# Softmax normalisation moved from the attention stage into the head of the merge, three logits tiles, keys loaded in quarters

## What is computed

```python
logits = jnp.einsum('bqgrd,bqkgd->bqgrk', q_b, k_sel).astype(jnp.float32) * att_scale
logits = jnp.where(valid[:, :, None, None, :], logits, NEG_INF)
p = jax.nn.softmax(logits, axis=-1)
return jnp.einsum('bqgrk,bqkgd->bqgrd', p.astype(v.dtype), v_sel)
...
gated = sigmoid(ga) * (y_att @ w_proj_att) + sigmoid(gm) * (y_mlstm @ w_proj_mlstm)
```

## Time and profile before

| | us |
|---|---|
| median of 3 runs | 3803.0 (3801.41 to 3805.9) |
| the profiled execution | 3799.4, span of the instructions 3797.8 |
| attention stage, first instruction to last result stored | about 1246 to 2107 |
| head of the merge | about 2107 to 2153 |

### The profile page before, as it was taken

How to read it: one execution, slowest core, us unless ns; L and a number is a source line. 1 busy time by engine, 2 the same in 40 slices (tenths; PEclk the granted TensorE clock), 3 DMA queues, 4 the chain that set the end, 5 groups by cost and what they waited for, 6 DMA issues and landing times. The chain is left out here.

```text
span 3797.8 us, 45544 instructions
## 1 busy us (share of the span) xinstructions
PE 3048.0 (80%) x12949; PEld 2294.5 (60%) x12950; DVE 2570.2 (68%) x3878; ACT 1789.7 (47%) x2406; POOL 478.1 (13%) x638
## 2 busy tenths in 40 slices
PE   3898699799999467878799495888179999999970
PEld 2766578587687234544455384767157777777760
DVE  4467689789899477767664333121379998989974
ACT  6222466585785223333333322121067777777750
POOL 0111110100000312111111000000311111111103
PEclk7999899999999689989899797888589999999995
DMA  2222322122122544333222454332067979667868
GB/s 99 71 63 72 101 78 83 53 77 83 53 74 68 120 102 92 94 98 78 75 66 46 154 173 151 105 120 90 24 223 255 352 281 352 225 245 262 304 241 354
DMA packets 347250, 537.33 MB, mean 141 GB/s; under 512 B 31508, under 2 KB 188404, under 8 KB 345588
## 3 DMA queue, kind: packets, MB, share of 16 engines
q1 hardware_dynamic: 314372, 422.80, 35.4%
q0 software_dynamic: 30448, 104.61, 7.4%
q10 hardware_dynamic: 2304, 8.39, 0.5%
HBM read 502.12 MB, written 138.47 MB: 169 GB/s over the span
## 5 line engine op out<-in xcount | busy, mean ns | idle before, releaser
L839 DVE TENSOR_TENSOR e_w_lo<-e_raw,e_w_hi 128x1024 fp32r<-128x1024 f32 x392 | 453.2, 1218 | 0.0
L1518 PE MATMUL x_ps<-h_hi,x_w_hi 128*128 128x512 f32 (+1 forms) x1024 | 402.4, 393 | 0.0
L1518 PE MATMUL x_ps<-h_lo,x_w_hi 128*128 128x512 f32 (+1 forms) x1024 | 401.1, 392 | 0.0
L1518 PE MATMUL x_ps<-h_hi,x_w_lo 128*128 128x512 f32 (+1 forms) x1024 | 400.8, 391 | 0.0
L791 ACT CAST e_w_hi<-e_raw 128x1024 fp32r<-128x1024 f32 x392 | 382.3, 1054 | 0.8 <-PE e_pG L742 0.7
L2218 ACT ACTIVATE t_probT<-t_ST 128x512 f32<-128x512 f32 x272 | 161.7, 595 | 357.7 <-PE t_ST L2064 357.2
L2037 PE MATMUL t_L<-t_k,t_q 128*128 128x512 f32 (+3 forms) x320 | 200.0, 665 | 147.2 <-DVE t_max_part L2243 112.1
L1708 DVE TENSOR_SCALAR_CACHE_REDUCE x_relu<-x_score,x_cand 128x1024 uint8<-128x1024 f32 (+3 forms) x217 | 315.6, 1486 | 3.6
L1621 ACT ACTIVATE x_relu<-x_score,x_cand 128x896 int8<-128x896 f32 (+3 forms) x217 | 281.0, 1296 | 55.5 <-DVE x_cand L1715 55.2
L2072 PE MATMUL t_O<-t_probT,t_v 128*128 128x512 f32 x544 | 298.2, 632 | 3.7 <-DVE t_y L2260 2.1
L2243 DVE CUSTOM_DVE_ANT_0 t_junk<-t_L,t_mask 128x512 bf16<-128x512 f32 (+3 forms) x320 | 186.7, 607 | 140.2 <-PE t_L L2037 138.3
(11 more groups left out here) (392 smaller groups left out, 6374.1 us busy)
## 6 DMA issues: line engine op xcount, KB each, us to landing
e_raw<-in_w_exp_gate SPq DMA_DIRECT2D x392, 256.0 KB
e_raw<-in_w_exp_up SPq DMA_DIRECT2D x392, 256.0 KB
e_raw<-in_w_exp_down SPq DMA_DIRECT2D x192, 512.0 KB
projT<-x_out SPq DMA_DIRECT2D x124, 256.0 KB, 2.7
slot_out<-e_y POOLq DMA_DIRECT2D x48, 512.0 KB, 5.9
b_gate<-projT SPq DMA_DIRECT2D x32, 512.0 KB, 5.2
x_w_raw<-in_w_in SPq DMA_DIRECT2D x31, 512.0 KB
x_t<-in_x SPq DMA_DIRECT2D x16, 512.0 KB
```

Of the source, the lines that this page charges most:

```text
L839: nc.vector.tensor_tensor(w_lo[:, u, :], raw[:, u, :], w_hi[:, u, :].bitcast(F32), ALU.subtract).then_inc(gl, 1)
L1518: last = nc.tensor.matmul(ps[0:w, u % 4, :], wt[:, m % 2, kk, 0:w], ht[:, kk, q * 512:(q + 1) * 512], start=(kk == 0 and s == 0), stop=(kk ...
```

## The change

- The value tile keeps 64 columns and one of ones, so `t_O` has 65 rows. It is one tile instead of two. At the end of a step ACT copies it (`out(s)`, behind the exponential of the next step's first unit) to one of three tiles `t_out`, and SP stores the 64 rows unnormalised (two DMAs) and the row of sums (one DMA) to DRAM, for each step, one unit later. `outputs` is gone from DVE.
- In the merge, the sums of all heads are loaded as one tile of 128x128, inverted at once, stored, and loaded again as `b_inverse`, each head's row repeated over 64 partitions (2 DMAs, 64x4x2048 each). The recurrence's four slices are taken first, then the attention's, which DVE multiplies with `b_inverse` before ACT's cast.
- `t_L` has three tiles, and PE may be three parts ahead of DVE.
- Keys and values are loaded in four quarters of 512 keys: the first before the second queries, the second at the end of the initial loads, the others at units 3 and 7. The stage's first loads are queries and keys, not gates. POOL fills one row of `t_k_shift` instead of 64, in two pieces.
- The gates' arithmetic moves from ahead of the units into units 0 to 14, and so do the waits for the convolution's weights. Chunks start at unit 32 instead of 30. Of a chunk, part of DVE's normalisation moves from offset 9 to 8, the transposes from 12 to 13, the result from 13 to 14, its store from 14 to 15. The first eight convolution units stand 2 to 3 units apart instead of 2.

```diff
@@ merge_branches @@
+    ORDER = [4, 5, 6, 7, 0, 1, 2, 3]
@@ sync @@
+            sp.dma_start(SUM[:, :], pg.d["exp_sums"]...).then_inc(sum_in, 16)
+            for at, k in enumerate(ORDER):
+                if at >= 2:
+                    sp.wait_ge(y_l, at - 1)
                 src = pg.d["y_attT" if k < 4 else "y_mlT"]
                 sp.dma_start(yr[:, k % 2, :], src[:, k % 4, :]).then_inc(y_in[k % 4], 16)
+                if at == 1:
+                    sp.wait_ge(rec_ok, 1)
+                    sp.dma_start(rec_d..., SUM[:, :]).then_inc(rec_st, 16)
+                    sp.wait_ge(rec_st, 16)
+                    for z in range(2):
+                        sp.dma_start(REC[z * AD:(z + 1) * AD, :, :], rec_d[z::2, :].partition_broadcast(AD)).then_inc(rec_in, 16)
@@ vector @@
+            dve.wait_ge(sum_in, 16)
+            nc.vector.reciprocal(SUM[:, :], SUM[:, :]).then_inc(rec_ok, 1)
+            for at, k in enumerate(ORDER):
+                if k < 4:
+                    dve.wait_ge(y_in[k], 32)
+                    dve.wait_ge(rec_in, 32)
+                    nc.vector.tensor_tensor(yr[:, k % 2, :], yr[:, k % 2, :], REC[:, k, :], ALU.mult).then_inc(n_ok, 1)
+                dve.wait_ge(y_h, at + 1)
                 nc.vector.tensor_tensor(y_lo[:, k, :], ...).then_inc(y_l, 1)
@@ attend_and_recur @@
-    CHUNK0, PERIOD = 30, 15
-    UNITS_AT = [1 + 2 * m if q == 0 else ...]
+    CHUNK0, PERIOD, NKC = 32, 15, 4
+    UNITS_AT = [1 + 5 * m // 2 if q == 0 else ...]
-        V = sb("v", [P, NT, AKV, P])
+        V = sb("v", [P, NT, AKV, AD + 1])
-        L = c.enter_context(nc.psum_tensor("t_L", [P, 2, 512], F32))
+        L = c.enter_context(nc.psum_tensor("t_L", [P, 3, 512], F32))
-        O = c.enter_context(nc.psum_tensor("t_O", [P, AKV, 512], F32))
+        O = c.enter_context(nc.psum_tensor("t_O", [P, R4, P], F32))
@@ sync @@
-            def store(n):
-                sp.wait_ge(y_ok, 2 * n + 2)
-                sp.dma_start(y_d[:, :, n * P:(n + 1) * P], Y[:, n % 2, :, :]).then_inc(y_st[n % 2], 16)
+            def store(s):
+                n, v = STEPS[s]
+                sp.wait_ge(ou_ok, s + 1)
+                for k in range(2):
+                    sp.dma_start(y_d[k * AD:(k + 1) * AD, 2 * v:2 * v + 2, n * P:(n + 1) * P],
+                                 OU[0:AD, s % 3, k::2, :]).then_inc(y_st[s % 3], 16)
+                sp.dma_start(sum_d[...], OU[AD:AD + 1, s % 3, :, :]).then_inc(y_st[s % 3], 16)
@@ tensor @@
-                if made >= 2:
-                    pe.wait_ge(mx_ok, made - 1)
+                if made >= 3:
+                    pe.wait_ge(mx_ok, made - 2)
@@ values @@
-                if j == 0 and s >= 2:
-                    pe.wait_ge(y_ok, s - 1)
-                nc.tensor.matmul(O[:, v, :], V[:, j, v, :], PT[:, (FIRST[s] + j) % 3, :], ...)
+                if j == 0 and s:
+                    pe.wait_ge(ou_ok, s)
+                nc.tensor.matmul(O[0:AD + 1, :, :], V[:, j, v, :], PT[:, (FIRST[s] + j) % 3, :], ...)
@@ scalar @@
+            def out(s):
+                act.wait_ge(pv_ok, FIRST[s + 1])
+                if s >= 3:
+                    act.wait_ge(y_st[s % 3], 48 * (s // 3))
+                a.copy(OU[:, s % 3, :, :], O[0:AD + 1, :, :]).then_inc(ou_ok, 1)
@@ vector @@
-            def outputs(s):
-                ...
-                v_.reciprocal(RS[:, v, :], O[AD:P, v, :]).then_inc(rs_ok, 1)
```

More of the change, by code:

```diff
@@ L181, in _ @@
         def _(act):
-            for k in range(8):
-                act.wait_ge(y_in[k % 4], 16 * (k // 4 + 1))
+            for k in ORDER:
+                if k < 4:
+                    act.wait_ge(n_ok, k + 1)
+                else:
+                    act.wait_ge(y_in[k % 4], 16)
                 nc.scalar.copy(y_hi[:, k, :], yr[:, k % 2, :]).then_inc(y_h, 1)
@@ L1791, in unit_at, with ended @@
         return UNITS_AT.index(f - off) if f - off in UNITS_AT else None
+    def ended(f, off):
+        return FIRST.index(f - off) - 1 if f - off in FIRST[1:] else None
     with ExitStack() as c:
@@ L1886, in load_chunk, with load_keys @@
                     sp.dma_start(to[:, b, :, :], rows.rearrange("(h c) n -> c h n", c=NT)[k].partition_broadcast(P)).then_inc(x_in[b], 16)
+            def load_keys(q):
+                part = slice(q * 512, (q + 1) * 512)
+                keys = pg.d["k_parts"].rearrange("s (v d) n -> s d v n", d=AD)[:, :, :, part]
+                for k in range(2):
+                    sp.dma_start(KS[k * AD:(k + 1) * AD, :, part].bitcast(F32), keys[k]).then_inc(k_in[q], 16)
+                sp.dma_start(K2[0:AD, :, part].bitcast(F32), keys[0]).then_inc(k_in[q], 16)
+                sp.dma_start(V[:, 4 * q:4 * q + 4, :, 0:AD], pg.d["v"][:, 4 * q:4 * q + 4]).then_inc(v_in[q], 16)
             rows = lambda at: pg.d["projT"][at:at + MH, :].rearrange("h (c n) -> (h c) n", n=P)
+            load(0)
+            load_keys(0)
+            load(1)
             sp.dma_start(gI[:, :], rows(C_IF)).then_inc(g_in, 16)
@@ L2163, in side @@
             def side(f):
-                if f == 7:
+                if f == 1:
+                    act.wait_ge(setup, 1)
+                    act.wait_ge(own_s, 2)
+                    a.activation(ge[:, :], gl[:, :], ACT.Exp, scale=-1.0).then_inc(g_ex, 1)
+                    act.wait_ge(g_ex, 1)
+                    a.activation(gl[:, :], ge[:, :], ACT.Ln, bias=one[:, :]).then_inc(g_ex, 1)
+                if f == 11:
                     act.wait_ge(g_w, 3)
@@ L2220, in _ @@
                         shift_row(s + 1)
+                    if j == 0 and s:
+                        out(s - 1)
                     side(f)
+            out(len(STEPS) - 1)
             for f in range(FLAT, FLAT + 20):
@@ L2378, in _ @@
                         seen, x = seen + 1, x + 1
-                    if j == 0 and s:
-                        outputs(s - 1)
                     if j == n and s + AHEAD < len(STEPS):
```

172 lines of the change are left out of this document (85 added, 87 removed).

## The result

The changed kernel took **3663.64 us** (median of 4 executions, 3660.08 to 3670.41), the kernel before, on the same chip, 3802.2. The ratio is 0.9638, 95% interval [0.9619, 0.9658]: 139 us less, faster, where 99 were forecast (3704 us). The time lies inside the range of 3650 to 3762. The profiled execution took 3666.89 us, its span is 3665.3 us.

What follows compares the result with a forecast made beforehand. PE was the engine to be fed, and DVE mostly failed to feed it. Terms -20 - 34 - 64 - 3 + 22 = -99 from 3799.4 us profiled gave 3700, plus 3.6 for the median: 3704 us, range 3650 to 3762.

Steps and rivals of the forecast that it cites:

- DVE's block at each step's end: Attention steps: a reciprocal of 64x512 and two products, 4.19 us per step, 134 us in all, taken off DVE.
- B: First 32 of 272 attention units (128 keys of one step each): less DVE work and PE idling, -34 us (-20 to -50).
- D: Drain after the last attention unit: a copy and two more DMA issues replace the last reciprocal, -3 us.
- A: Attention stage filling its buffers, up to the first exponential: fewer loads ahead, -20 us (-12 to -28).
- the bias wait: Buffer filling: DVE stood until 1289.59 for the convolution bias, needed only later; the change puts this wait behind the maxima.
- C: The other 240 attention units: shorter PE waits and higher granted clock, 660 to 596 us, -64 (-30 to -95).
- the maxima: PE's waits for DVE's maxima in the last 240 units: 58.1 us before, 25 left.
- the GpSimd product: PE's wait in the recurrence, last 240 units, caused by a 15 us load: 30 of 48.6 us left.
- the output tile: Step boundaries: with one tile, the next value product waits for ACT's copy; 7 us for 31 boundaries (0 to 19).
- E: Head of the merge, PE empty: loading repeated inverse rows and DVE's serial work add +22 us (+16 to +115).
- PE is fed almost fully: Rival, 15%: third tile and freed DVE take nearly all waits for maxima, clock stays 1.00; -151 us, 3652 us.
- The repeated rows load slowly: Rival, 5%: the merge's 4.19 MB load at 44 GB/s, 95 us instead of 11; 3788 or 3841 us.

Runs made afterwards that it cites:

- packed rows: Changed kernel with each chunk's four repeated rows of 512 B side by side in DRAM instead of 8 KB apart; ratio 0.9618.
- DVE's load back: Changed kernel with a reciprocal of 64x512 and two products put back on DVE at each step's end, results unused; ratio 0.9848.
- padded rows: Changed kernel with each chunk's four repeated rows of 512 B lying 9.5 KB apart in DRAM instead of 8 KB; ratio 0.9614.

## Why the prediction was right, and where it was off

**Direction, range and mechanism.** Right: of the named causes DVE's block at each step's end starved PE the most (80 us when it is put back), the third tile smooths (15), the move of the chunks' last steps counts (25). The sum was off by 40 us, and no stretch but B and D came out within 3 us.

**A, -27 for -20.** The last load that the logits of the first four steps waited for was there at 1266.59, close to the 1268 of the forecast:

```profile
1266.59 1.01 PE L2078 MATMUL t_L<-t_k,t_q 128*128 128x256 f32 x3 [1.69 <-DMA t_q_shift<-q_parts]
```

From there to the first exponential it took 6.3 us instead of 10.4, and of the 2 us for ACT's tables nothing was seen (the one table load there, 1.28 us at 1271.12, lay under PE's products). Its other two parts came out as summed: 12 us from the loads (13 in the trace, 1279.73 to 1266.59) and 10 from the bias wait. But the term treats A and B as separate, and they trade: 9.6 of the 14.6 us that the quartered keys give come back in B.

**B, -32 for -34.** Right in size. I charged 7 us for the loads there; the run with all loads ahead puts them at 9.6. The way was another, and in part this is luck: the sum counted the gates' arithmetic as 9 us of DVE's work and not the two trips through DRAM inside it, which hold PE for 6.47 + 5.05 us, and DVE's work came to 72.7 us instead of 77.

**C, -94 for -64: the mis-sized term.** The sum was 509 of work + 62 idle + 25 missing clock. Measured: 515 of work, 40 idle (566.2 - 526.3) and 11 missing clock (0.02 of 526). 22 of the 30 us are idle time and 14 the clock, less 6 us more work. The 509 had 6 us of idle time in them, since PE's idle time before was 113 us (660 - 547) and the sum took off 107.

Of the three waits that the forecast named, the maxima were to keep 25 us and kept 11.0, the GpSimd product was to keep 30 and kept 12.3, and the output tile was to cost 7 and cost 0.7: 24 us where 62 stood. Against that stand 15.6 us of waits for ACT's exponentials, which the sum put at nothing. The largest miss is in the amount left for the GpSimd product, 30 of 48.6. Its mechanism was read rightly. It hangs on the load of the rows (packed rows take the last 12.3 us away), and more work on DVE does not lengthen it (8.7 us with DVE's load back). What was mis-sized is what a unit of slack does: with the last steps one unit earlier the wait is 28.1 us, with them in place 12.3. Why it is 28.1 there and no longer 48.6, with the chunks starting at unit 32, was not tried alone. The clock lost less than in proportion to the idle time: by the forecast's own 44 to 107, 40 us of idle time would cost 16, and they cost 11.

**D, -3 for -3.** Right.

**E, +28 for +22.** The third slice was cast 32.8 us after the head's start instead of 14.0: +18.8, where +10.5 and 2 for the small transfers stood. The step that failed is "at the 380 GB/s of rows of this size": the rate was taken from slices over 128 partitions, and the two new loads write 64 each, 208 GB/s, 20 us for 11. The second half of the term, DVE's serial cycle, came to 41.2 us from there to PE's first product instead of 31.5, +9.7 for +9.6. This match is partly luck: the cycle took 6.46 us, not 6.9, and DVE waited 2.44 us for the first attention slice, which the term did not have. The errors of C and E have opposite signs, so the total hides some of each.

**Slips in its figures.** The prediction speaks of eight loads for a chunk; they are six. Its bound of +115 for E doesn't follow from its own terms: 95 us instead of 11 is 84 more, on +22, so +106. Neither moves the forecast.

**The rivals.** "PE is fed almost fully" came closest, with C at -95, A at -26 and 3652 us; it had 15%. It missed on B (-45) and on E (+18). "The repeated rows load slowly" was right that they are slow and wrong in cause and size: 208 GB/s, not 44, by the partitions they go to and not by the repetition. The sentence that the Trainium skill ("DMA: Bandwidth & Descriptors", Rules for kernel authors) could not settle this term stands: both loads have the outermost dim that the page asks for, and neither slow rate here comes from it (415 GB/s over 128 partitions, 4.9 us with padded rows, with such a dim outermost too). That the trace disagrees with the page was said too strongly: a share of 0.15 tells how busy the engines are, not how many take part.

## What to carry to other kernels

When a busy block of 4 us is taken off an engine that stands ahead of TensorE in a chain, count more than the waits that it shortens: a microsecond of DVE was worth 0.6 us here, and in the trace half of that came as longer products at a lower granted clock. When work with a trip through DRAM in its middle is moved in among the units, count the trip as well: the two trips here left DVE idle for 5.85 and 4.91 us. Before a DMA's rate is taken from another row, compare the partitions that it writes and the distance of its pieces in DRAM, not only their size. A step that is the last of a serial chain deserves a unit of slack before anything in it is made faster.

## What was not expected of the hardware

Rows of 512 B that lie 8 KB apart, read by all 128 partitions, landed after 10.3 us; at 9.5 KB apart after 4.9, and in pieces of 2 KB side by side also after 4.9. A transfer to 64 partitions kept all DMA engines busy (share 1.01) at 208 GB/s, one to 128 at 415; here the share of busy DMA engines says nothing of the rate. And in TensorE's idle head of the merge, 16 products of 16x512, 7.9 us in all, were enough work to replace 4.19 MB of DMA (beside four slice buffers and a new order), although the granted clock stayed at 0.50, the lower level (1.2 GHz), throughout.
